# HGRN scores as blocks of 64 tokens in two column halves, and the next chunk's first two levels scaled ahead

## What is computed

```python
def _hgrn2_scan(q, k, i, logf):
    '''S_t = diag(f_t) S_{t-1} + k_t i_t^T (k_t = 1 - f_t), o_t = S_t^T q_t.'''
    ...
    def step(state, inp):
        q_n, k_n, i_n, b_n = inp
        dec = jnp.exp(jnp.where(incl, b_n[:, :, :, None, :] - b_n[:, :, None, :, :], -jnp.inf))
        att = jnp.einsum('bhtd,bhsd,bhtsd->bhts', q_n, k_n, dec)
        o = (jnp.einsum('bhtd,bhdv->bhtv', q_n * jnp.exp(b_n), state)
             + jnp.einsum('bhts,bhsv->bhtv', att, i_n))
        ...
```

## Time and profile before

| | us |
|---|---|
| median of 3 runs | 3058.03 (3057.94 to 3058.41) |
| the profiled execution's own time | 3055.75 |
| its span | 3053.9 |
| PE busy in the span | 2895.9 |
| DVE busy | 1478.1 |
| ACT busy | 1158.5 |
| POOL busy | 1008.4 |
| HGRN stage of layer 1, first to last product | 399.4 to 524.6 |
| HGRN stage of layer 2 | 1461.7 to 1586.9 |

### The profile page before, as it was taken

How to read it: one execution, slowest core, us unless ns; L and a number is a source line. 1 busy time by engine, 2 the same in 40 slices (tenths; PEclk the granted TensorE clock), 3 DMA queues, 4 the chain that set the end, 5 groups by cost and what they waited for, 6 DMA issues and landing times. The chain is left out here.

```text
span 3053.9 us, 40768 instructions
## 1 busy us (share of the span) xinstructions
PE 2895.9 (95%) x16854; PEld 2387.6 (78%) x16854; DVE 1478.1 (48%) x2014; ACT 1158.5 (38%) x1813; POOL 1008.4 (33%) x540
## 2 busy tenths in 40 slices
PE   6988998999999989989989999999898999999999
PEld 4788988878888767889878788887576767788887
DVE  4565557427616345655574376263493552441120
ACT  3562643323313236536433233132333652342232
POOL 2263021014534423630210145343342323344433
PEclk9999999999999999999999999999989999999999
DMA  5102201333423231022023334232522222333332
GB/s 163 37 22 69 70 1 57 96 104 90 120 73 100 66 111 56 3 69 70 1 70 93 100 90 118 75 102 57 121 69 58 77 62 78 94 94 94 95 90 76
DMA packets 419833, 235.81 MB, mean 77 GB/s; under 512 B 24020, under 2 KB 416706, under 8 KB 419010
## 3 DMA queue, kind: packets, MB, share of 16 engines
q1 hardware_dynamic: 419650, 233.20, 26.9%
HBM read 226.88 MB, written 6.29 MB: 76 GB/s over the span
## 5 line engine op out<-in xcount | busy, mean ns | idle before, releaser
L2014 POOL TENSOR_TENSOR WLO<-RAW,WHI 128x1024 fp32r<-128x1024 f32 (+1 forms) x205 | 533.6, 2608 | 984.6 <-ACT WHI L1895 984.6
L144 PE MATMUL PS<-HHI,WHI 128*128 128x512 f32 x2016 | 798.2, 396 | 24.3 <-POOL HLO L563 14.6
L145 PE MATMUL PS<-HLO,WHI 128*128 128x512 f32 x2016 | 790.4, 392 | 0.0
L146 PE MATMUL PS<-HHI,WLO 128*128 128x512 f32 x2016 | 790.2, 392 | 0.0
L144 PEld LDWEIGHTS PS<-HHI,WHI 128*128 128x128 f32 x2016 | 381.0, 189 | 118.2 <-POOL HLO L563 16.2
L145 PEld LDWEIGHTS PS<-HLO,WHI 128*128 128x128 f32 x2016 | 380.6, 189 | 83.1 <-issue 2.7
L146 PEld LDWEIGHTS PS<-HHI,WLO 128*128 128x128 f32 x2016 | 380.5, 189 | 82.2
L1895 ACT CAST WHI<-RAW 128x1024 fp32r<-128x1024 f32 (+1 forms) x208 | 227.4, 1098 | 550.1 <-PE PS L146 538.4
L2008 DVE TENSOR_TENSOR X<-X,PS 128x512 f32<-128x512 f32 x48 | 32.9, 687 | 372.4 <-PE PS L146 372.4
L144 PE MATMUL PS<-MHI,WHI 128*128 128x512 f32 x384 | 154.4, 402 | 16.0 <-DVE WLO L1967 11.1
L1991 DVE SCALAR_TENSOR_TENSOR ACC<-GP,PARS,ACC 128x512 f32<-128x512 f32 x88 | 162.8, 1850 | 3.1
(11 more groups left out here) (449 smaller groups left out, 5125.2 us busy)
## 6 DMA issues: line engine op xcount, KB each, us to landing
RAW<-in_w_up SPq DMA_DIRECT2D x88, 512.0 KB, 3.8
RAW<-in_w_in SPq DMA_DIRECT2D x82, 512.0 KB, 4.0
RAW<-in_w_mlp SPq DMA_DIRECT2D x64, 512.0 KB, 4.0
RAW<-in_w_down SPq DMA_DIRECT2D x32, 704.0 KB, 4.5
RAW<-in_w_in SPq DMA_DIRECT2D x20, 1024.0 KB, 5.3
RAW<-in_w_gate SPq DMA_DIRECT2D x32, 512.0 KB, 4.1
RAW<-in_w_out SPq DMA_DIRECT2D x24, 512.0 KB, 4.1
x_kept<-X SPq DMA_DIRECT2D x2, 2048.0 KB, 9.3
```

The source lines that it names most:

```text
L144: e.matmul(out, wh, xh, start=first and n == 0, stop=False)
L145: e.matmul(out, wh, xl, start=False, stop=False)
L146: last = e.matmul(out, wl, xh, start=False, stop=final and n == len(quads) - 1)
L2014: pool.tensor_tensor(slot(WLO, u), source(u), slot(WHI, u), ALU.subtract).then_inc(lo_s, 1)
```

## The change

The score tile is no longer gathered at 128 x 128. For the diagonal and the levels 0 to 5 each head's product is made as two products, one for each block of 64 columns of the same X tile: contraction over all 128 channels, 64 columns of weights, 64 moving columns, and 64 partitions written (the first block's scores go to partitions 0 to 63, the second's to 64 to 127, at the same columns). So both lie in 256 columns instead of 512 for the four heads. DVE gathers them, with masks of half the width (`MASK`, `EYE`, built by DVE at the start of the stage), into a new tile `AC` of 128 x 4 x 64. Level 6 has a routine of its own, `last_level`: one product for each lane and head, which gives the 64 x 64 block across the halves.

ACT has a new step, `assembled`: four copies (two lanes, two halves) from `AC` to the diagonal blocks of `AT`, and one for each lane from PSUM to the corner block of level 6. The other corner is set to zero once by DVE. `outputs` waits for ACT (`af`) where it waited for DVE (`ac`). DVE no longer gathers level 6.

DVE scales level 0 and level 1 of chunk m+1 after the gathers of chunk m and ahead of the state sums; before, level 0 came behind them and level 1 behind the diagonal.

```diff
@@ hgrn_stage
+    W = 64
+    HALVES = (slice(0, W), slice(W, P))
+    FIRST, SECOND = HALVES, HALVES[::-1]
+    MASK, EYE = new("hMASK", [P, 2, LEVELS - 1, W]), new("hEYE", [P, W])
+    for d in lanes:
+        B[d]["AC"] = new(f"hAC{d}", [P, 4, W])
...
+        small = lambda d, n: acc(d, n)[:, 0:4 * W].rearrange("p (h n) -> p h n", h=4)
@@ diagonal
-                        last = pe.matmul(ha(d, 1, h), kt_of(m, d)[:, h, :], q_of(m, d)[:, h, :], start=True, stop=True)
+                        for rows in HALVES:
+                            last = pe.matmul(small(d, 1)[rows, h, :], kt_of(m, d)[:, h, rows], q_of(m, d)[:, h, rows], start=True, stop=True)
@@ level
                     for h in H4:
-                        last = pe.matmul(ha(d, n, h), x[:, h, :], x[:, h, :], start=True, stop=True)
+                        for rows in HALVES:
+                            last = pe.matmul(small(d, n)[rows, h, :], x[:, h, rows], x[:, h, rows], start=True, stop=True)
                     last.then_inc(S["a"][d], 1)
+
+                def last_level(m):
+                    n = LEVELS - 1
+                    for d in lanes:
+                        pe.wait_ge(S["x"][d], 2 * (m * LEVELS + n + 1))
+                        pe.wait_ge(S["ac"][d], m * n + n - 1)
+                    for h in H4:
+                        for d in lanes:
+                            x, one, two = B[d][f"X{n % 2}"], FIRST[d], SECOND[d]
+                            last = pe.matmul(small(d, n)[one, h, :], x[:, h, one], x[:, h, two], start=True, stop=True)
+                            if h == 3:
+                                last.then_inc(S["a"][d], 1)
@@ outputs
-                    pe.wait_ge(S["ac"][d], (m + 1) * LEVELS)
+                    pe.wait_ge(S["af"][d], m + 1)
@@ ACT
+                def assembled(m):
+                    for d in lanes:
+                        act.wait_ge(S["mk"][0], 3)
+                        act.wait_ge(S["ac"][d], (m + 1) * (LEVELS - 1))
+                        if m:
+                            act.wait_ge(S["o"][d], m)
+                        for rows in HALVES:
+                            act.copy(B[d]["AT"][rows, :, rows], B[d]["AC"][rows])
+                    for d in lanes:
+                        one, two = FIRST[d], SECOND[d]
+                        act.wait_ge(S["a"][d], (m + 1) * LEVELS)
+                        act.copy(B[d]["AT"][one, :, two], small(d, LEVELS - 1)[one]).then_inc(S["af"][d], 1)
...
                         decays(m + 1, 1, 0)
+                    assembled(m)
+                    if m + 1 < CH:
                         decays(m + 1, 0, 1)
@@ DVE
-                    dve.copy_predicated(B[d]["AT"][:, :, :], mask(PAIR + d * LEVELS + n), per_head(acc(d, n))).then_inc(S["ac"][d], 1)
+                    dve.copy_predicated(B[d]["AC"][:, :, :], heads(MASK[:, d, n, :], 4).bitcast(I32), small(d, n)).then_inc(S["ac"][d], 1)
+
+                for rows in HALVES:
+                    dve.tensor_copy(EYE[rows, :], C[rows, IDENT, rows])
+                    for d in lanes:
+                        at = PAIR + d * LEVELS
+                        last = dve.tensor_copy(MASK[rows, d, :, :], C[rows, at:at + LEVELS - 1, rows])
+                    last.then_inc(S["mk"][0], 1)
+                for d in lanes:
+                    last = dve.memset(B[d]["AT"][SECOND[d], :, FIRST[d]], 0.0)
+                last.then_inc(S["mk"][0], 1)
+                for n in range(2):
+                    for d in lanes:
+                        scaled(0, d, n)
                 for m in range(CH):
                     for d in lanes:
-                        scaled(m, d, 0)
-                    for d in lanes:
                         dve.wait_ge(S["dia"][d], m + 1)
-                        if m:
-                            dve.wait_ge(S["o"][d], m)
-                        dve.tensor_tensor(B[d]["AT"][:, :, :], per_head(acc(d, 1)), heads(C[:, IDENT, :], 4), ALU.mult).then_inc(S["diac"][d], 1)
+                        dve.wait_ge(S["af"][d], m) if m else dve.wait_ge(S["mk"][0], 3)
+                        dve.tensor_tensor(B[d]["AC"][:, :, :], small(d, 1), heads(EYE[:, :], 4), ALU.mult).then_inc(S["diac"][d], 1)
                     for n in range(LEVELS):
-                        if n + 1 < LEVELS:
+                        if 0 < n < LEVELS - 1:
                             for d in lanes:
                                 scaled(m, d, n + 1)
-                        for d in lanes:
-                            gather(m, d, n)
+                        if n < LEVELS - 1:
+                            for d in lanes:
+                                gather(m, d, n)
+                    if m + 1 < CH:
+                        for n in range(2):
+                            for d in lanes:
+                                scaled(m + 1, d, n)
```

More of the change, by code:

```diff
@@ L1301, in hgrn_stage @@
         B[d].update({n: new(f"h{n}{d}", [P, 512], F32R) for n in ("FH", "FL")})
+    W = 64
[4 more added lines that the diff above has]
+        B[d]["AC"] = new(f"hAC{d}", [P, 4, W])
     last_col = (P - 1, 0)
-    kinds = ("fh", "fl", "kt", "ktc", "suf", "es", "g", "e", "dia", "diac", "x", "a", "ac", "qe", "kd", "sd", "o", "oc", "oa", "st", "su")
+    kinds = ("mk", "af", "fh", "fl", "kt", "ktc", "suf", "es", "g", "e", "dia", "diac", "x", "a", "ac", "qe", "kd", "sd", "o", "oc", "oa", "st", "su")
     with signals.stage(*[f"hgrn_{n}{d}" for n in kinds for d in lanes]) as sems:
@@ L1402, in level @@
                     if n >= 2:
-                        pe.wait_ge(S["ac"][d], m * LEVELS + n - 1)
+                        pe.wait_ge(S["ac"][d], m * (LEVELS - 1) + n - 1)
                     elif n == 1:
@@ L1443, in _ @@
                     for n in range(LEVELS):
-                        for d in lanes:
-                            level(m, d, n)
+                        if n < LEVELS - 1:
+                            for d in lanes:
+                                level(m, d, n)
+                        else:
+                            last_level(m)
                         if n == 0:
@@ L1514, in _ @@
             def _(dve):
-                mask = lambda n: heads(C[:, n, :], 4).bitcast(I32)
                 def scaled(m, d, n):
@@ L1530, in gather @@
                     if n:
-                        dve.wait_ge(S["ac"][d], m * LEVELS + n)
+                        dve.wait_ge(S["ac"][d], m * (LEVELS - 1) + n)
                     else:
                         dve.wait_ge(S["diac"][d], m + 1)
-                    dve.copy_predicated(B[d]["AT"][:, :, :], mask(PAIR + d * LEVELS + n), per_head(acc(d, n))).then_inc(S["ac"][d], 1)
+                    dve.copy_predicated(B[d]["AC"][:, :, :], heads(MASK[:, d, n, :], 4).bitcast(I32), small(d, n)).then_inc(S["ac"][d], 1)
```

## The result

| | before | changed |
|---|---|---|
| median, us | 3057.99 | 3033.34 |
| lowest and highest of 4 runs | 3057.15 to 3058.41 | 3031.88 to 3035.47 |
| profiled execution's span | 3053.9 | 3029.9 |

A forecast was written before the change was run, and what follows sets the result against it. PE's work was taken to bound chunks 0 to 2, DVE chunk 3. Chunks of 22.0, 24.5, 24.9 and 20.5 with 9.7 ahead made 101.6 us a stage instead of 125.2, 47.2 less for two layers: 3010.8 us, range 3002 to 3030.

The forecast's parts named there:

- The batch at 0.93 us: PE's diagonal and level products: 32 records of 64 columns at 0.029 us each, the two column halves side by side.
- the drains at 0.33 us for an excursion: PE changing between product shapes: 0.33 us each time, five times a chunk, 1.65 us.
- level 6: PE's last level in a chunk: 16 records alternating between the lanes' halves, 0.47 us.
- Rivals 1 and 2: PE's column halves: one after the other, 3052 us, chance 0.06; or weight loads not hidden, about 3150 us, chance 0.05.
- rival 2: PE's column halves: each record costs its load and its stream, about 0.112 us; about 3150 us in all, chance 0.05.
- DVE's gathers: Gathers of half the width on DVE: 0.27 us off each, from 0.62 to 0.35 apart.
- ACT: Assembly copies at a chunk's end: 2.2 us, of which 0.2 shows in chunks 0 to 2 and 2.1 in chunk 3.
- rival 3: Chunk end: ACT's decays and copies run late, outputs wait for `af`, up to 2.2 us a chunk; 3023 us, chance 0.09.
- The level scaled ahead: DVE's early scaling, 2.7 us, lies wholly under PE's work; level 2's scaling inherits POOL's delay, 0.5 us in chunks 1 and 2.
- The step that failed: FL for the next chunk, wanted earlier: POOL's two operations may make PE wait 0.5 us in chunks 1 and 2 (0 to 2).
- "The granted clock still 1.00": Sign that the forecast is right: PE's granted clock stays at 1.00, as in all the stage's windows before.
- the start: Before the first diagonal: DVE builds masks beside POOL's FL, which may cost 0 to 1.3 us, taken as 0.5.

The follow-up runs named there:

- fl_short: The change with POOL making only 16 of FL's 512 columns from the second chunk on, that work left out; 3020.20 us.
- ahead_only: The kernel before with only the scaling of levels 0 and 1 ahead of the state sums, full products and gathers kept; 3050.92 us.
- filler: The change with products of no use on PE in its waits, ahead of level 3 in chunks 0 to 2 and in chunk 3; 3024.15 us.
- fill_last: The change with the products of no use on PE in chunk 3 alone; 3025.67 us.
- fl_short_fill: The change with FL cut to 16 columns from the second chunk on and products of no use in chunk 3; 3011.29 us.

## Why the prediction was half right

- **PE's products: right.** The batch at 0.93 us, the drains at 0.33 us for an excursion and level 6 held; fl_short's chunks at 22.5, 24.9 and 24.3 us are their check, and the rounds of chunk 3 start 2.0 us apart, 2.04 by the forecast. Rivals 1 and 2 are refuted by the first batch. The Trainium skill, TensorEngine Tiling (Array Packing), Key Properties, says that a change of tiling mode drains the engine; the trace agrees, with 3.12 us for a batch and its exponents where 0.93 and 1.92 make 2.85. The Trainium skill, TensorE: Matmul & The Clock Gate, Part 3, lets a weight load overlap products in flight only for other row groups, which would have made rival 2 true; the trace doesn't agree, at 2.08 us for 64 records of the same rows.
- **DVE's gathers: right**, 445 ns, where 737 was the length before and 0.45 us the forecast.
- **ACT: right.** Outputs follow the exponents within 0.3 us in chunks 1 and 2, and rival 3 didn't come. In chunk 3 PE waits 1.6 us for `af`.
- **The level scaled ahead: right in its place.** Its gain appeared, and level 2's scaling did inherit POOL's QE, KD and SD. DVE paid 1.8 us for it in chunk 1 and 0.9 in chunk 2, and of this PE waited 0.3 us in chunk 1 (2.36 us for the 64 records of levels 1 and 2 instead of 2.08); 0.5 was taken. But the forecast looked for turns between DVE and POOL there and at level 0 alone.
- **The step that failed** is the one on FL. The forecast saw that "level 3 comes about 8 us into a chunk instead of 12", and from that it priced only PE's own wait for FL ("POOL's two operations ... may make PE wait 0.5 us in chunks 1 and 2"). That wait didn't come: PE waits for FL at the start of the stage alone, 1.4 us before and after. What FL does to DVE's scaling of level 3 stands nowhere in the sum, in none of the chunks. It is a missing term of 2.0, 1.6 and 2.1 us in chunks 0, 1 and 2 of each layer, 11.4 us in all; fl_short measured 13.1 with the clock's share. The kernel before had a sign of it, which none of the rows showed: in its chunk 0 one scaling beside FL took 1.50 us and PE waited 0.76 us behind it. In its chunks 1 and 2 the same two engines met at levels 2 and 3 with the other outcome; this is chunk 2:

```profile
478.17 0.42 DVE L1525 TENSOR_TENSOR hX<-HQ,hE 128x256 f32<-128x256 f32 x1
478.22 4.44 POOL L1335 TENSOR_TENSOR hFL<-LF,hFH 128x512 fp32r<-128x512 f32 x2 [5.04 <-ACT hFH L1467]
478.51 0.42 DVE L1526 TENSOR_TENSOR hX<-RAW,hE 128x256 f32<-128x256 f32 x1
478.84 1.36 DVE L1534 COPY_PREDICATED hAT<-C,PS 128x512 f32<-128x512 int32 x2
```

  and this is chunk 2 of the change:

```profile
468.33 0.41 DVE L1563 TENSOR_TENSOR hX<-HQ,X 128x256 f32<-128x256 f32 x1
468.37 2.91 POOL L1343 TENSOR_TENSOR hFL<-LF,hFH 128x512 fp32r<-128x512 f32 x2 [1.80 <-ACT hFH L1492]
468.66 1.49 DVE L1564 TENSOR_TENSOR hX<-RAW,X 128x256 f32<-128x256 f32 x1
```

  In both, POOL began 0.04 or 0.05 us behind the start of a scaling, and DVE had no gap. Before, DVE kept its 0.42 us and POOL's two operations took 4.44 us; in the change POOL's take 2.91 and DVE pays. The short products aren't needed for that: ahead_only has the full ones, and in its chunks 1 and 2 FL takes 2.68 us and a scaling 1.48. What decides who pays stays open. The Trainium skill, GPSIMD Engine Reference, Key points, says that GpSimd shares its SBUF interfaces with DVE and that DVE operations with two SBUF inputs contend for them; the trace agrees in that gathers, whose data come from PSUM, kept their length beside POOL (0.76 us for the pair at 440.28, beside FL, and for the pair at 443.85, behind it).
- **"The granted clock still 1.00": wrong.** It fell in both layers' chunk 3 and in three more chunks of layer 1. filler prices it at 9.2 us in all, fill_last at 7.7. In the profiled executions chunk 3 is 2.8 us shorter in each layer with the products of no use, and chunks 0 to 2 of the change's layer 1 are 4.5 us longer than those of its layer 2; this second part is not there in every execution. The forecast had computed that PE would wait for DVE in chunk 3 and drew no conclusion for the clock. The slow end of the range took in only delays of the forecast's own kind, and was too near by 3 us.
- **Luck.** That fl_short_fill meets the forecast to 0.5 us is partly luck: the start cost 0.1 us and not 0.5, PE didn't wait for FL, chunks 0 and 1 are 0.5 and 0.4 longer than forecast and chunk 2 is 0.6 shorter.

## What to carry to other kernels

When one engine's work is made shorter, list again which engines work beside each other: two operations that took turns where nobody waited can land on the new critical stretch, and a sum over durations doesn't show it. If two parts of a change gain 8 us each alone and 25 together, look for an obstacle that both share and for what of it still stands in the way. Here it was worth 16 us to move 1.4 us of subtraction a chunk from POOL to DVE. Where a stage passes from being bound by PE to having holes of 2 us on PE, price the products behind the holes at the lower clock too, as a term that may or may not come.

## What the runs showed of the hardware

- Two fp32 products that share all 128 rows of the array and differ only in their 64 columns run side by side: 32 records of 64 columns in about 1.15 us from first start to last end, against 1.95 us for 16 full ones.
- When a DVE operation with two SBUF inputs meets a POOL operation, either can be the one that waits: 1.4 to 1.5 us on DVE instead of 0.42 with POOL at 1.3 each, or 2.2 us each on POOL with DVE at 0.42. In chunk 2 of both kernels POOL began just behind a scaling and DVE had no gap, and the two outcomes differ.
- Behind a wait of 2.3 us on PE the granted clock was 0.58 in the mean from 418.0 to 421.4, and 0.51 over chunk 3's outputs; behind the same wait in layer 2, and in fill_last, it was 1.00. With products that compute nothing in the waits it was 1.00 in all four chunks, and the kernel 9 us faster.
